# Output projection of a fused two-block kernel: two tiles move ahead of the last transposes of attention, and the sums of squares follow two tiles behind instead of one

## The chip, the cores and the metric

The kernel runs on one core of one Trainium2 chip. The metric is the time of one execution on the device, in microseconds (us). Three executions were timed before the change: 3608.86, 3610.43 and 3611.48 us, median 3610.43 us. One more execution was recorded by the profiler; its own time was 3605.72 us and the span from its first to its last instruction 3604.4 us.

## What is computed

Two transformer blocks, each on 1024 tokens of width 1024, all in fp32. The first mixes tokens with grouped attention, a Hyena convolution and differential attention, projects the result with `w_out`, adds it (scaled by a gate) to the residual and goes into a gated MLP. The second is a three-part attention mixer and a mixture of experts. The change lies in the step of the first block between attention and MLP:

```python
def merge_groups(ya, yh, yd, g_out, w_out, lam_init):
    ya = rms_norm(ya, g_out[:A_WIDTH])
    yh = rms_norm(yh, g_out[A_WIDTH:A_WIDTH + HY_WIDTH])
    yd = rms_norm(yd, g_out[A_WIDTH + HY_WIDTH:].reshape(D_HEADS, D_VALUE_DIM)) * (1.0 - lam_init)
    return jnp.concatenate([ya, yh, yd.reshape(b, n, D_WIDTH)], axis=-1) @ w_out
...
# then, in the block: x = x + gate * y; h = rms_norm(x, norm2_g), modulated; the MLP reads h
```

## The kernel before, in words

Every engine has its own generator of instructions (`pe_...`, `act_...`, `dve_...`, `sp_...`). A generator yields the name of an event that it needs, such as `("yt", 7, 1)`, and gets the semaphore and the count to wait for; so the order on each engine is the order of its own code, and only semaphores tie the engines together. Two of the tools matter here: `claim(b)` makes TensorE wait until PSUM bank `b` has been read by its last user (`held[b]`), and `ring` hands out banks in turn.

**Attention** works through 48 units: for each of 8 query tiles of 128 tokens two units of grouped attention and four of differential attention. When a query tile `qt` is complete, it is normalised in small steps between the units: VectorE copies the Hyena part in (L1148), ScalarE squares and sums six groups (L1086), takes a reciprocal square root (L302, L304, each with a table load), VectorE refines it (L308 to L312) and scales the six groups (L1161, event `("yn", qt)`). Then TensorE turns the eight 128x128 blocks of the tile to feature-major layout (`pe_features`, L1032, in two PSUM banks), and ScalarE copies them to `YT` with the output gain (`act_norm`, L1098, event `("yt", qt, h2)`). For the last query tile, 7, there are no more units between which these steps could go. A query tile of the Hyena part lands on every second token, tiles 0 to 3 and 4 to 7 in the first and in the second 512 tokens.

**Output projection** (`pe_wout`). There are 16 tiles of 128 features x 512 tokens, in the order of `halves`: the first 512 tokens (tc = 0) for features 0 to 7, then the second 512. They are called T0 to T15 here. A tile is 8 matmuls in the code, each of which the profile shows as two rows (fp32), so 16 rows on L1237; it goes to the next of banks 0 to 5. T0 to T7 read only the first 512 columns of `YT`. VectorE then adds the tile, times the gate, to the residual (`dve_wout`, L1253, event `xadd`), which SyncE loads from DRAM in eight transfers of 512 KB (L1197, `xres`) into memory that held the attention's operands. ScalarE squares the sum (`act_wout`, L1272, event `rsq`) into one of two buffers that it uses in turn; TensorE adds the squares over the features with a matmul by a constant (`pe_wout_sum` by way of `pe_column_sum`, L1221, two rows, event `rss`), into bank 6 for the first token half and bank 7 for the second. These are called S0 to S15. In the order before, S(i-1) stands behind Ti. When S7 is there, VectorE and ScalarE make the factors of the first half (L1256, L302, L304, L308 to L312) and the normalised input of the MLP (L1261, L1278), and only then go on with T8; likewise after S15, on which the MLP (`pe_glu`, L1298) waits.

**Weights** come in chunks of 1 MB through four slots (L197); a chunk of `w_out` serves two tiles. The first two chunks are loaded during attention, the third and fourth when the last attention unit no longer reads their slots. SyncE then waits for `("yt", 7, 1)`, issues the eight residual loads, and goes on with the chunks for T8 to T15.

The lines of the order before: TensorE waits for `("yt", 7, 1)` ahead of all tiles (L1230), `pe_features(7, ttb)` ends `pe_attention` (L1055).

Of the kernel before, what the change touches and what calls it, by code (L numbers as in the profile page):

```python
# [85 lines left out]
class Turns:  # L86
# [9 lines left out]
    def turn(self, *events):  # L96
        i = self.i
        self.i = (i + 1) % len(self.sems)
        self.counts[i] += 16
        for event in events:  # L100
            self.engine.at[event] = (self.sems[i], self.counts[i])
        return self.sems[i], 16
# [21 lines left out]
def build(nc, X, out):  # L124
# [4 lines left out]
    V, A, G, P, S = (Engine(nc, e, n, at) for e, n in ((vt, "dve"), (st, "act"), (gt, "pool"), (nc.tensor, "pe"), (dma, "sp")))  # L129
# [3 lines left out]
    def sb(off, n, p0=0, p1=128):  # L133
        assert off + n <= TOTAL
        return arena[p0:p1, off:off + n]
# [13 lines left out]
    def bk(b, n=512, p0=0, p1=128, off=0):  # L149
        return psum[p0:p1, b, off:off + n]  # L150
# [14 lines left out]
    def claim(*banks):  # L165

        for b in banks:
            for event in held[b]:
                P.wait_ge(*(yield event))
            held[b] = []  # L170

    def ring(ids):
        i = 0
        while True:
            yield ids[i % len(ids)]
            i += 1
# [8 lines left out]
    def wat(n):  # L185
        return M_WR + (n % NWR) * WSZ

    def wready(n):
        return wsem[n % NWR], 16 * (n // NWR + 1)
# [770 lines left out]
    def grouped(i):  # L960
        return i is not None and 0 <= i < NU and units[i][0] == "a"
# [13 lines left out]
    def norm_step(i):  # L975
        return divmod(i - 8, 6) if i > 7 else (0, -1)

    def pe_scores(i):
        kind, qt, h = units[i]
        q, key = (QA, KA) if kind == "a" else (QD, KD + h * 1280)  # L980
        yield from claim(*range(6))
        for c, n in ((0, 512), (512, 512), (1024, 256)):
            for j in range(2):
                ins = mm(bk(3 * j + c // 512, n), sb(q + h * 1024 + qt * 128, 128, 64 * j, 64 * j + 64), sb(key + c, n, 64 * j, 64 * j + 64), True, True)  # L984
                if c == 1024:
                    ins.then_inc(*P.step(("score", i, j)))
        for b in range(6):
            held[b] = [("cmax", i, b // 3)]

    def pe_turn(i, j, ttb):  # L990
        P.wait_ge(*(yield ("exp", i, 1) if units[i][0] == "a" else ("comb", i)))
        for g in range(3):
            b = next(ttb)
            yield from claim(b)
            for k in range(4 * g, min(10, 4 * g + 4)):
                ins = turn(bk(b, 128, off=k % 4 * 128), prob(i, j)[:, k * 128:k * 128 + 128], ident)  # L996
            bank[("turn", i, j, g)] = b
            ins.then_inc(*P.step(("turn", i, j, g)))
            held[b] = [("pt", i, j, g)]

    def pe_values(i, ttb):
        kind, qt, h = units[i]
        b = next(ttb)
        yield from claim(b)
        for j in range(2 if kind == "a" else 1):
            P.wait_ge(*(yield ("pt", i, j, 2)))
        for k in range(10):
            if kind == "a":
                for j in range(2):
                    ins = mm(bk(b, 128, 64 * j, 64 * j + 64), sb(VA + k * 128 + 64 * j, 64), probt(i, j, k * 128, 128), k == 0, k == 9)  # L1010
            else:
                ins = mm(bk(b, 128), probt(i, 0, k * 128, 128), sb(VD + k * 512 + h * 128, 128), k == 0, k == 9)  # L1012
        bank[("val", i)] = b
        ins.then_inc(*P.step(("val", i)))
        held[b] = [("yt4", i) if kind == "a" else ("y", i)]

    def pe_back(i, ttb):
        b = next(ttb)
        yield from claim(b)
        P.wait_ge(*(yield ("yt4", i)))  # L1020
        bank[("back", i)] = b
        turn(bk(b, 128), sb(YA, 128), ident).then_inc(*P.step(("back", i)))
        held[b] = [("y", i)]

    def pe_features(qt, ttb):
        y = YTK + qt % 2 * 1024
        P.wait_ge(*(yield ("yn", qt)))
        for h2 in range(2):
            b = next(ttb)
            yield from claim(b)  # L1030
            for k in range(4):
                ins = turn(bk(b, 128, off=k * 128), sb(y + (4 * h2 + k) * 128, 128), ident)  # L1032
            bank[("feat", qt, h2)] = b
            ins.then_inc(*P.step(("feat", qt, h2)))
            held[b] = [("yt", qt, h2)]

    def pe_attention():
        ttb = ring([6, 7])
        P.wait_ge(*(yield ("lam",)))
        P.wait_ge(*(yield ("qv", NJ - 1)))  # L1040
        P.wait_ge(*(yield ("qk", roped[-1])))
        for i in range(NU + 3):
            if i < NU:
                yield from pe_scores(i)
            if 2 <= i < NU + 2:
                yield from pe_turn(i - 2, 0, ttb)
            if i > 2:
                yield from pe_values(i - 3, ttb)
            if grouped(i - 4):
                yield from pe_back(i - 4, ttb)  # L1050
            if grouped(i - 2):
                yield from pe_turn(i - 2, 1, ttb)
            if norm_step(i)[1] == 5:
                yield from pe_features(norm_step(i)[0], ttb)
        yield from pe_features(7, ttb)  # L1055

    def act_turn(i, j):
        x = side_of[i, j]
# [130 lines left out]
    halves = [(tc, f) for tc in range(2) for f in range(8)]  # L1189
# [27 lines left out]
    def pe_column_sum(tile, ready, done, tc, f):  # L1217
        if f == 0:
            yield from claim(6 + tc)
        P.wait_ge(*(yield ready))  # L1220
        mm(bk(6 + tc), con("o1024"), tile, f == 0, f == 7).then_inc(*P.step(done))  # L1221

    def pe_wout_sum(tc, f):
        yield from pe_column_sum(sb(SQ + f % 2 * 512, 512), ("rsq", tc, f), ("rss", tc, f), tc, f)
        if f == 7:
            held[6 + tc] = [("rx", tc)]

    def pe_wout():
        banks = ring(range(6))
        P.wait_ge(*(yield ("yt", 7, 1)))  # L1230
        for tc, f in halves:
            n = nth["wout"][4 * tc + f // 2]
            b = next(banks)
            yield from claim(b)
            P.wait_ge(*wready(n))
            for k in range(8):
                ins = mm(bk(b), sb(wat(n) + k * 256 + f % 2 * 128, 128), sb(YT + k * 1024 + tc * 512, 512), k == 0, k == 7)  # L1237
            bank[("wout", tc, f)] = b
            ins.then_inc(*P.step(("wout", tc, f), *([("w", n)] if f % 2 else [])))
            held[b] = [("xadd", tc, f)]  # L1240
            if f:
                yield from pe_wout_sum(tc, f - 1)
            elif tc:
                yield from pe_wout_sum(0, 7)
        yield from pe_wout_sum(1, 7)

    def dve_wout():
# [1503 lines left out]
    def pe_program():  # L2751
        P.stage("front")
        yield from pe_front()
        P.stage("hyena")
        yield from pe_hyena()
        P.stage("qkv")
        yield from pe_qkv()
        P.stage("attention")
        yield from pe_attention()
        P.stage("ffn")  # L2760
        yield from pe_wout()
        yield from pe_glu()
        yield from pe_down()
        P.stage("band")
        yield from pe_band()
        P.stage("mla")
        yield from pe_mla()
        P.stage("wout2")
        yield from pe_wout2()
        yield from pe_route()  # L2770
        P.stage("experts")
        yield from pe_experts()
        yield from pe_final()
# [247 lines left out]
```

## Time and profile before

| what | value |
|---|---|
| three executions, median (lowest to highest) | 3610.43 us (3608.86 to 3611.48) |
| profiled execution, its own time | 3605.72 us |
| its span | 3604.4 us |
| TensorE busy with matmuls | 3410.5 us, 95% of the span |
| VectorE, ScalarE, GpSimd busy | 1569.7, 901.0, 261.8 us |
| mean granted TensorE clock | 0.98 of full speed |
| output projection, first row of L1237 to last of L1221 | 1058.4 to 1193.4 us |

The profile gives each instruction's start and duration, what the engine waited for ahead of it, and the granted TensorE clock; a matmul of one row is about 0.43 us from the last at 512 columns and full clock. The ends of matmuls are modelled and overlap the next start a little, so pitches are read from starts.

### The profile page before, as it was taken

The page shows a single profiled execution, that of the slowest core. Times are in us where ns is not written, and L with a number is a line of the kernel's source. Part 1 is how long each engine was busy: PE and PEld are TensorE (multiplying, and loading weights), DVE is VectorE, ACT ScalarE, POOL GpSimd, SP SyncE. Part 2 cuts the span into 40 slices and gives each one's busy share as a digit, 9 for nine tenths or more (in the row PEclk, how much of TensorE's full clock was granted, in tenths as well). Part 3 has the DMA queues.
Part 4 walks back from the last instruction along what each step waited for, and adds up shares of the span by engine and source line. Part 5 has one row for each costly group of instructions (what it writes and reads, how often), then busy time and mean ns, then how long its engine had stood idle before and what let it go on. Part 6 is the DMA issues. An engine that isn't in the chain of part 4 may idle for free.

```text
span 3604.4 us, 30844 instructions
## 1 busy us (share of the span) xinstructions
PE 3410.5 (95%) x12338; PEld 1861.5 (52%) x12338; DVE 1569.7 (44%) x2766; ACT 901.0 (25%) x1750; POOL 261.8 (7%) x251
## 2 busy tenths in 40 slices
PE   8999998899989899999999999999999987999997
PEld 3458545666654344444444555765457434444443
DVE  6355476466631555554543213314666133211114
ACT  4110363377751100000000112213334121111112
POOL 0012232000000000000000000000000002222221
PEclk9999999999999999999999999999999998999999
DMA  6124212000022211110210200002000108999994
GB/s 231 35 70 160 98 47 105 24 1 1 1 82 82 70 38 45 47 47 29 87 47 24 85 24 30 31 7 91 12 24 1 49 24 353 370 370 366 370 369 168
DMA packets 63242, 370.56 MB, mean 103 GB/s; under 512 B 6826, under 2 KB 13242, under 8 KB 37500
## 3 DMA queue, kind: packets, MB, share of 16 engines
q1 hardware_dynamic: 40492, 187.71, 14.3%
q0 software_dynamic: 22608, 180.89, 13.3%
q8 instruction: 97, 1.59, 0.2%
q14 instruction: 45, 0.37, 0.0%
HBM read 329.16 MB, written 39.41 MB: 102 GB/s over the span
## 4 chain that ended last, share of the span: by engine, by line
PE 83%; DVE 7%; ACT 7%; DMA 1%; issue 1%; SPq 0%; POOL 0%; DVEq 0%; ACTq 0%; POOLq 0%
PE ps L1298 15%; PE ps L2568 9%; PE ps L1421 7%; PE ps L1596 6%; PE ps L2587 4%; PE ps L837 3%; PE ps L2225 3%; PE ps L1237 3%; PE ps L1598 3%; PE ps L984 2%; PE ps L703 2%; PE ps L840 2%; PE ps L1012 2%; PE ps L646 2%; ACT arena L1064 2%; PE ps L2065 2%
## 5 line engine op out<-in xcount | busy, mean ns | idle before, releaser
L1298 PE MATMUL ps<-arena 128*128 128x512 f32 x1232 | 532.1, 594 | 9.4 <-DVE arena L1324 9.4
L1298 PEld LDWEIGHTS ps<-arena 128*128 128x128 f32 x1232 | 234.3, 190 | 307.0 <-issue 287.1
L2568 PE MATMUL ps<-arena 128*128 128x512 f32 x752 | 331.1, 593 | 0.0
L1421 PE MATMUL ps<-arena 128*128 128x512 f32 x616 | 264.6, 592 | 0.0
L2526 POOL DMA_INDIRECT arena<-in_wgu_dram,arena x47 | 44.2, 940 | 2639.7 <-DVE arena L2485 2387.5
L2568 PEld LDWEIGHTS ps<-arena 128*128 128x128 f32 x752 | 139.6, 191 | 157.7 <-issue 157.7
L1596 PE MATMUL ps<-arena 128*128 128x512 f32 x480 | 209.1, 596 | 0.0
L1421 PEld LDWEIGHTS ps<-arena 128*128 128x128 f32 x616 | 116.6, 189 | 147.9 <-issue 143.8
L1119 DVE TENSOR_SCALAR_CACHE_REDUCE arena<-ps 128x1280 f32<-128x1280 f32 x96 | 139.3, 1488 | 110.1 <-PE ps L984 110.1
L837 PE MATMUL ps<-arena 128*128 128x512 f32 (+1 forms) x432 | 174.7, 558 | 0.0
L2587 PE MATMUL ps<-arena 128*128 128x512 f32 x376 | 169.1, 592 | 0.5 <-DVE arena L2638 0.5
L2642 DVE TENSOR_TENSOR arena<-arena,ps 128x256 f32<-128x256 f32 x47 | 19.8, 421 | 323.6 <-ACT arena L2613 323.6
L1596 PEld LDWEIGHTS ps<-arena 128*128 128x128 f32 x480 | 90.8, 190 | 113.8 <-issue 113.8
L1077 ACT ACTIVATE arena<-arena 128x1280 f32<-128x1280 f32 x96 | 129.5, 1353 | 7.0 <-DVE arena L1119 7.0
L984 PE MATMUL ps<-arena 64*128 64x512 f32 (+1 forms) x576 | 119.7, 547 | 6.8 <-DVE arena L1119 3.1
L837 PEld LDWEIGHTS ps<-arena 128*128 128x128 f32 x432 | 82.1, 191 | 84.7 <-issue 82.5
L1613 DVE COPY arena<-ps 128x512 f32<-128x512 f32 (+2 forms) x31 | 16.6, 536 | 247.5 <-PE ps L1596 157.7
L996 PE MATMUL ps<-arena 128*128 128x128 f32 x640 | 100.0, 285 | 24.3 <-ACT arena L1064 21.0
L2587 PEld LDWEIGHTS ps<-arena 128*128 128x128 f32 x376 | 71.4, 190 | 90.2 <-issue 89.4
L1237 PE MATMUL ps<-arena 128*128 128x512 f32 x256 | 115.9, 607 | 1.4 <-ACT arena L1098 1.4
L1064 ACT ACTIVATE arena<-ps 128x512 f32<-128x512 f32 (+1 forms) x192 | 93.8, 523 | 85.9 <-PE ps L996 83.5
L2225 PE MATMUL ps<-arena 128*128 128x512 f32 x256 | 112.5, 592 | 0.7 <-DVE arena L2195 0.7
(375 smaller groups left out, 4940.9 us busy)
## 6 DMA issues: line engine op xcount, KB each, us to landing
arena<-in_wmod_dram SPq DMA_DIRECT2D x24, 1024.0 KB, 5.5
yslot<-arena SPq DMA_DIRECT2D x47, 512.0 KB, 9.1
arena<-in_wup_dram SPq DMA_DIRECT2D x22, 1024.0 KB, 4.8
arena<-in_wout_dram SPq DMA_DIRECT2D x16, 1024.0 KB, 4.8
arena<-in_cf_dram SPq DMA_DIRECT2D x12, 1024.0 KB, 4.8
arena<-in_wdn_dram SPq DMA_DIRECT2D x16, 704.0 KB, 4.0
arena<-in_w2b_dram SPq DMA_DIRECT2D x9, 1024.0 KB, 4.8
arena<-in_ci_dram SPq DMA_DIRECT2D x16, 512.0 KB, 3.5
```

What stands on the lines that cost most here:

```text
L837: ins = mm(bk(b, size), sb(wat(n) + k * 256 + col, 128), x, k == 0, k == 7)
L984: ins = mm(bk(3 * j + c // 512, n), sb(q + h * 1024 + qt * 128, 128, 64 * j, 64 * j + 64), sb(key + c, n, 64 * j, 64 * j + 64), True, True)
L1064: st.activation(probt(i, j, g * 512, n), bk(bank[("turn", i, j, g)], n), ACT.Copy).then_inc(*A.step(("pt", i, j, g)))
L1077: st.activation(prob(i, j), prob(i, j), ACT.Exp, bias=stat(i, f"bias{j}"), scale=-1.0, accum_out=stat(i, f"sum{j}")).then_inc(*A.step(("ex ...
L1119: vt.tensor_scalar(prob(i, j), scores(j), -SCALE, None, MUL, ALU.min, accum_out=stat(i, f"bias{j}")).then_inc(*V.step(("cmax", i, j)))
L1237: ins = mm(bk(b), sb(wat(n) + k * 256 + f % 2 * 128, 128), sb(YT + k * 1024 + tc * 512, 512), k == 0, k == 7)
L1298: ins = mm(bk(b), left[:, k], right[:, k], k == 0, k == 3)
L1421: ins = mm(bk(b), sb(left + k * 128, 128), right(k), k == 0, k == 10)
L1596: ins = mm(bk(b), sb(w, 128), sb(x + tile * 512, 512), k == 0, k == 7)
L2225: ins = mm(bk(b), sb(wat(n) + k * 256 + f % 2 * 128, 128), sb(OF + k * 1024 + tc * 512, 512), k == 0, k == 7)
L2568: ins = mm(bk(b), sb(XB + i % 2 * 1024 + k * 128, 128), sb(WGU[i % 3] + k * 512, 512), k == 0, k == 7)
L2587: ins = mm(bk(6 + h2), sb(HB + 512 + i % 2 * 256 + k * 128, 128), sb(WDN[i % 4] + k * 1024 + h2 * 512, 512), k == 0, k == 1)
```

## The change

TensorE's order alone changes. The transposes of query tile 7 leave the end of `pe_attention` and stand behind T1; T0 to T7 wait for query tile 6 (`("yt", 6, 1)`) instead of 7, T8 to T15 still for tile 7; the transposes take a new ring of banks 6 and 7. S(i-2) instead of S(i-1) stands behind Ti, from T2 on, and S14 and S15 close the projection. The code of the other engines is the same.

```diff
                 yield from pe_turn(i - 2, 1, ttb)
             if norm_step(i)[1] == 5:
                 yield from pe_features(norm_step(i)[0], ttb)
-        yield from pe_features(7, ttb)
...
     def pe_wout():
         banks = ring(range(6))
-        P.wait_ge(*(yield ("yt", 7, 1)))
-        for tc, f in halves:
+        for i, (tc, f) in enumerate(halves):
+            P.wait_ge(*(yield ("yt", 7 if tc else 6, 1)))
             n = nth["wout"][4 * tc + f // 2]
             b = next(banks)
             yield from claim(b)
...
             held[b] = [("xadd", tc, f)]
-            if f:
-                yield from pe_wout_sum(tc, f - 1)
-            elif tc:
-                yield from pe_wout_sum(0, 7)
+            if i == 1:
+                yield from pe_features(7, ring([6, 7]))
+            if i > 1:
+                yield from pe_wout_sum(*halves[i - 2])
+        yield from pe_wout_sum(1, 6)
         yield from pe_wout_sum(1, 7)
```

One line falls away above `pe_wout`, so the line numbers behind it are lower by one after the change.

TensorE, from the values of the last attention unit (L1012) on, before. L1032 are the transposes, L1237 the projection, L1221 the sums; `attention_act` and `ffn_act` are ScalarE's semaphores, `attention_dve` and `ffn_dve` VectorE's, `weights0` to `weights3` the four slots:

```order
L1012 MATMUL ps<-arena 128x128 [waits attention_act]
L1012 MATMUL ps<-arena 128x128 x9
L1032 MATMUL ps<-arena 128x128 [waits attention_act,attention_dve]
L1032 MATMUL ps<-arena 128x128 x7
L1237 MATMUL ps<-arena 128x512 [waits weights0,attention_act]
L1237 MATMUL ps<-arena 128x512 x15
L1221 MATMUL ps<-arena 128x512 [waits ffn_act]
L1237 MATMUL ps<-arena 128x512 [waits weights1]
L1237 MATMUL ps<-arena 128x512 x7
L1221 MATMUL ps<-arena 128x512 [waits ffn_act]
```

And the same place after:

```order
L1012 MATMUL ps<-arena 128x128 [waits attention_act]
L1012 MATMUL ps<-arena 128x128 x9
L1236 MATMUL ps<-arena 128x512 [waits weights0,attention_act]
L1236 MATMUL ps<-arena 128x512 x15
L1031 MATMUL ps<-arena 128x128 [waits attention_dve]
L1031 MATMUL ps<-arena 128x128 x7
L1236 MATMUL ps<-arena 128x512 [waits weights1]
L1236 MATMUL ps<-arena 128x512 x7
L1220 MATMUL ps<-arena 128x512 [waits ffn_act,attention_act]
L1236 MATMUL ps<-arena 128x512 x8
```

T0 and T1 (x16 matmuls) went ahead of the eight transposes, and S0 went from behind T1 to behind T2, where it also waits for ScalarE's reading of the bank that the transposes used.

TensorE at the end of the projection, where L1298 (L1297 after) is the first product of the MLP, before:

```order
L1221 MATMUL ps<-arena 128x512 [waits ffn_act]
L1237 MATMUL ps<-arena 128x512 [waits ffn_dve]
L1237 MATMUL ps<-arena 128x512 x7
L1221 MATMUL ps<-arena 128x512 [waits ffn_act] x2
L1298 MATMUL ps<-arena 128x512 [waits weights0,ffn_dve]
```

And after:

```order
L1220 MATMUL ps<-arena 128x512 [waits ffn_act]
L1236 MATMUL ps<-arena 128x512 [waits ffn_dve]
L1236 MATMUL ps<-arena 128x512 x7
L1220 MATMUL ps<-arena 128x512 [waits ffn_act] x3
L1297 MATMUL ps<-arena 128x512 [waits weights0,ffn_dve]
```

Three sums instead of two stand behind T15.

## Rows read from the trace of the kernel before

**Rows 1.** The page: busy time of the engines, and the chain that ended last.
```profile
PE 3410.5 (95%) x12338; PEld 1861.5 (52%) x12338; DVE 1569.7 (44%) x2766; ACT 901.0 (25%) x1750; POOL 261.8 (7%) x251
...
PE 83%; DVE 7%; ACT 7%; DMA 1%; issue 1%; SPq 0%; POOL 0%; DVEq 0%; ACTq 0%; POOLq 0%
```

**Rows 2.** Waits of TensorE, 1040 to 1200 us: us in total, times, longest.
```profile
PE ps L1032 <- DVE arena L1161: 8.9, 1, 8.9
PE ps L1221 <- ACT arena L1272: 6.1, 2, 5.5
PE ps L1237 <- ACT arena L1098: 1.4, 1, 1.4
```

**Rows 3.** Timeline of TensorE: start, us, instructions [idle before <- releaser].
```profile
1041.83 1.27 PE L1032 MATMUL ps<-arena 128*128 128x128 f32 x8
1043.67 2.50 PE L1012 MATMUL ps<-arena 128*128 128x128 f32 x20 [0.57 <-ACT arena L1098]
1055.04 1.97 PE L1032 MATMUL ps<-arena 128*128 128x128 f32 x8 [8.88 <-DVE arena L1161]
1058.42 16.73 PE L1237 MATMUL ps<-arena 128*128 128x512 f32 x32 [1.41 <-ACT arena L1098]
1074.99 1.02 PE L1221 MATMUL ps<-arena 128*128 128x512 f32 x2
1075.85 7.03 PE L1237 MATMUL ps<-arena 128*128 128x512 f32 x16
1082.71 1.02 PE L1221 MATMUL ps<-arena 128*128 128x512 f32 x2
```

**Rows 4.** Stretches: us, busy us (x) by engine, then PEclk, DMA share, GB/s.
```profile
1046.20:1055.00 8.80, 0.00 (x0) 0.00 (x0) 3.06 (x14) 5.61 (x16) 0.00 (x0) 0.73 0.64 238
1058.40:1062.00 3.60, 3.58 (x5) 1.51 (x6) 0.00 (x0) 0.00 (x0) 0.00 (x0) 0.50 0.73 229
1062.00:1064.00 2.00, 2.00 (x4) 0.97 (x3) 0.00 (x0) 0.00 (x0) 0.00 (x0) 0.51 1.01 399
```

**Rows 5.** Timeline of ScalarE, VectorE and SyncE's queue around the first tiles.
```profile
1042.47 2.18 ACT L1098 ACTIVATE arena<-ps,arena 128x128 f32<-128x128 f32 x8 [2.75 <-PE ps L1032]
1056.19 2.18 ACT L1098 ACTIVATE arena<-ps,arena 128x128 f32<-128x128 f32 x8 [3.45 <-PE ps L1032]
...
1068.40 0.75 DVE L1253 SCALAR_TENSOR_TENSOR arena<-ps,arena 128x512 f32<-128x512 f32 x1 [13.41 <-PE ps L1237]
...
1069.19 0.63 ACT L1272 ACTIVATE arena<-arena 128x512 f32<-128x512 f32 x1 [10.82 <-DVE arena L1253]
...
1058.40 3.76 SPq L1197 DMA_DIRECT2D arena<-in_xT_dram  x8
```

**Rows 6.** TensorE at S8, between the halves, and at the end of the projection.
```profile
1142.41 2.08 PE L1221 MATMUL ps<-arena 128*128 128x512 f32 x2 [5.45 <-ACT arena L1272]
1144.28 7.83 PE L1237 MATMUL ps<-arena 128*128 128x512 f32 x16
...
1190.58 1.02 PE L1221 MATMUL ps<-arena 128*128 128x512 f32 x2
1192.24 1.13 PE L1221 MATMUL ps<-arena 128*128 128x512 f32 x2 [0.65 <-ACT arena L1272]
```

**Rows 7.** Residual loads: the issues at 1058.8 and 1059.2; then landing of all.
```profile
L1197 SPq DMA_DIRECT2D arena<-in_xT_dram x2: 431/432/432, 1058.8 to 1059.2; - x2
...
DMA to landing us min/median/max: 5.5/5.5/5.5
...
DMA to landing us min/median/max: 5.5/7.5/9.4
```

**Rows 8.** The page: issues of `w_out` chunks, KB each, median us to landing.
```profile
arena<-in_wout_dram SPq DMA_DIRECT2D x16, 1024.0 KB, 4.8
```

**Rows 9.** TensorE after a short wait late in attention, 1033 to 1038 us.
```profile
1033.44 0.69 PE L996 MATMUL ps<-arena 128*128 128x128 f32 x2 [2.06 <-ACT arena L1064]
1033.93 3.78 PE L1012 MATMUL ps<-arena 128*128 128x128 f32 x20
```

## The prediction

> **What bounds the kernel.** First the page: TensorE is busy 95% of the span, and the chain that ended last runs through it for 83% [rows 1]. VectorE and ScalarE are busy 44% and 25%, so they matter only where TensorE waits for them. Hence the second view, TensorE's waits in the stretch of the change. There are four in 160 us that cost a microsecond or so: 8.9 us ahead of the last transposes, for VectorE's scaling of query tile 7; 1.4 us ahead of T0, for ScalarE's copies of those transposes; and 5.5 us and 0.65 us ahead of S8 and S15, for squares [rows 2, 6]. Third, the timeline gives their places [rows 3]: the last values of attention end at 1043.67 + 2.50 = 1046.17 us, the transposes begin at 1055.04, T0 at 1058.42, T2 at 1075.85. Fourth, the granted clock [rows 4]: over the wait it falls from full to half (mean 0.73 over 1046.2 to 1055.0), and is still at 0.50 in T0's first 3.6 us and 0.51 in the 2 us behind. These are the levels of 1.2 and 2.4 GHz.
>
> Everything behind the projection (MLP, band attention, routing, experts) is released by its result, in the same order on all engines. So what TensorE gains up to S15 should reach the end, unless a transfer or the clock takes it back.
>
> **The wait ahead of the transposes.** T0 and T1 need the first 512 tokens of `YT` (query tile 6 and those before it), their first weights, and banks 0 and 1. Tile 6's copies end at 1042.47 + 2.18 = 1044.65 us [rows 5]; the weights were loaded during attention; the banks were last read by the maxima of the last scores, long before the values. So T0 can start when the values end, at 1046.1. The idle 8.88 us are filled.
>
> T0 and T1 take two tiles at full clock. A warm tile is 1082.71 - 1075.85 = 6.86 us, two are 13.72 [rows 3]. They end at about 1059.9, later than 1055.0, when tile 7 is ready, so the transposes wait for nothing. The clock was full ahead of 1046 (20 rows in 2.50 us, which took 3.78 us at the low clock [rows 3, 9]) and finds no idle stretch now. Before, the pair took 1074.99 - 1058.42 = 16.57. Gain 2.85 us. The transposes took 1.97 us slow and 1.27 us for tile 6 at full clock [rows 3]: gain 0.70 us.
>
> **The wait ahead of T0.** The 1.41 us for ScalarE's copies are gone: what follows the transposes now is T2, which needs only tile 6 and its weights. Gain 1.41 us.
>
> **What becomes later.** The transposes run at 1059.9 instead of 1055.0. The copies start when the first four are done, at about 1060.5 (0.64 us behind, as 1042.47 - 1041.83 shows), and end 2.18 us later at 1062.7; before, at 1058.4. SyncE's queue waits for just this with the eight residual loads, and behind them the weights of T8 to T15. These move by 4.3 us against the clock on the wall, and by some 19 us against T2, which starts at 1061.2 instead of 1075.85. For the weights that is covered: T8 begins some 46 us after T2, and such a chunk lands in 4.8 us [rows 8]. For the residual it has to be worked out, because S0 stands behind T2 and needs load, addition and square of T0. T2 ends at 1061.2 + 6.86 = 1068.0. The third load, issued at 1059.24, landed 5.5 us later at 1064.7 [rows 7]; loads follow each other at 512 KB / 399 GB/s = 1.3 us [rows 4], so the first landed about 2.6 us before it, at 1062.1, or 3.7 us after the first issue. Now that is 1062.7 + 3.7 = 1066.4; addition 0.75 and square 0.63 us, with 0.04 us between each [rows 5], give 1067.9. The stall at S0 is about nothing; I take 0.1 us. The bounds are 0 and what it would be if the first load took as long as the last, 9.4 us [rows 7]: 5.6 us. From S1 on there is a whole tile more.
>
> **Sums two behind.** No sum is added or removed; each is 0.86 us (1075.85 - 1074.99). Ahead of T15's end there is one fewer (S0 to S12 instead of S0 to S13), behind it one more. Before, S15 began 1192.24 - 1190.58 = 1.66 us after T15's end, 0.65 us of it idle while T15's addition and square ran [rows 6]. Now S13 and S14, 1.72 us, stand there and fill the idle time; the square also waits for S13, since there are two buffers, but that ends 0.86 us in, about when the addition ends. Gain 0.86 - 0.06 = 0.80 us.
>
> The wait at S8 I leave as it is. It comes from VectorE, which makes the first half's norm between S7 and T8's addition. Before, the order is S7, T9, S8; now S7, T10, S8. One tile lies between in both, so 5.45 us stay, with the slow clock behind it: S8 takes 2.08 and the next tile 7.83 us [rows 6]. Banks don't change that: T14, the first tile to reuse T8's, comes four tiles after T10.
>
> ScalarE's squares get a later release: the square of Ti needs S(i-2), now issued behind Ti instead of T(i-1). That is ready 0.86 us after Ti, the addition 0.8 to 0.95 us after it, so nothing moves, and the result is needed a tile later than before.
>
> **Sum.** 8.88 + 1.41 + 2.85 + 0.70 + 0.80 - 0.1 = 14.5 us. Against the profiled execution: 3605.72 - 14.5 = 3591.2 us. That execution was 4.7 us faster than the median of the three timed ones (3610.43) and below the fastest, so for a timed median I take 3610.4 - 14.5 = **3595.9 us**.
>
> **The clock, weighed.** After a wait of 2.06 us, 20 rows took 3.78 instead of 2.50 us [rows 3, 9]; after the 0.57 us ahead of the values nothing slowed; after the 5.45 us at S8 the loss was 1.22 + 0.80 = 2.0 us; after 8.88 and 1.41 us, 3.55 us. So the loss isn't in proportion to the wait. The Trainium skill, "TensorE: Matmul & The Clock Gate", section "What's actually happening", says that the window in which activity is judged runs freely and doesn't restart with the kernel's work, so where a stretch lies in it decides how much runs slow. By that rule the waits behind the projection, all moved by 14.5 us, may each cost a little more or less than in this trace, and the sum would be 14.5 give or take a few us rather than 14.5. No row here shows the same wait at two phases, only unequal losses.
>
> **Rivals.**
> 1. *The residual comes late.* S0 waits for the first load as if it took the last's 9.4 us: 5.6 us, and such a wait brings 2 us of slow clock, as at S8. Gain 14.5 - 5.5 - 2.0 = 7.0, time 3603.4; halfway it is 3599.6. For it: the third load took 5.5 us, and this is the one place where slack falls from a tile and more to about zero. Against it: loads land at an even spacing, which puts the first at 3.7 us. Chance 0.10.
> 2. *The clock takes or gives.* The later waits meet the clock otherwise. By the losses above each moves by up to 2 us; three in one direction make 6 us: 3602 or 3590. For it: the unequal losses. Against: signs should differ. Chance 0.06.
> 3. *It does nothing:* T0 does not start early, because a count it waits for is reached only with tile 7. Then T0 would wait as before; 3610. Against it: the wait is for tile 6's copies, and ScalarE ran them before the values ended [rows 5]. Chance 0.03.
> 4. *Slower.* The two square buffers tie TensorE and ScalarE together: a sum finds its square not made and waits for the chain addition, square, that behind T15 is 1.66 us from the tile's end [rows 6]. At 15 sums that is 24.9 us; less 14.5 it is 10.4 slower, 3620.8. It decides against the change if more than 8 to 9 of the sums wait so. Against it: the chain is 1.7 us long and S(i-2) comes more than 14 us after its tile's end (two tiles). Chance 0.01.
>
> **How the numbers follow.** A measurement of this kernel can tell about 0.2%, or 7.2 us, from no change; faster means below 3603.2. The forecast has 0.80; its own range, with 2 us on each side for the clock and 1.5 us for executions (they spread by 2.6 us), is 3592.5 to 3599.5. The rivals 1 and 2 reach to 3603.4 and 3590. For 8 in 10 with some doubt about my own terms I give 3591.5 to 3602.0. Faster 0.80 + 0.09 + 0.05 = 0.94; same 0.01 + 0.01 + 0.03 = 0.05; slower 0.01.
>
> **What the profile after would show.** T0 starting within 0.3 us of the values' end, at clock 1.00; transposes with no wait of VectorE, taking about 1.3 us; no wait ahead of T2; S0 waiting under 0.5 us; S8 waiting about 5.5 us still, some 14 us earlier; three sums in a row at the end with no idle time; S15 at about 1177.7 instead of 1192.2. Wrong would be: a wait of microseconds at S0, T0 at a low clock, or a projection that ends 14 us sooner while the whole is not 14 us shorter.

## The result, and the profile after

The changed kernel's five timed executions have a median of 3590.9 us (3589.77 to 3594.19), five of before in the same job 3610.43 us (3608.37 to 3611.48). The ratio is 0.9944, with a 95% interval of 0.9934 to 0.9955. The profiled execution took 3590.90 us, its span 3589.6 us. That is 14.8 us less than the profiled execution of before, but 19.5 us less between the medians. The forecast was 3595.9 us. It was right in direction and, as the rows below show, in what happens in the projection; the result lies 5.0 us under it and 0.6 us under the lower end of its range, 3591.5. What is to be explained is therefore not the projection but these 5 us.

The page of the changed kernel, to be read against [rows 1]:

```profile
PE 3406.6 (95%) x12338; PEld 1858.3 (52%) x12338; DVE 1569.4 (44%) x2766; ACT 900.4 (25%) x1750; POOL 261.8 (7%) x251
```

The same instructions; TensorE is busy 3.9 us less, since fewer of them run at the low clock. The other 10.9 us of the span were idle time.

TensorE's timeline of the changed kernel, in the columns of [rows 3, 6]. L1236 is the projection, L1220 the sums, and the row of x8 at 128x128 the transposes. These are on L1032 and the MLP's first product is on L1298, as before; the lists of the order ahead of the prediction, which give L1031 and L1297 for them, are one line off:

```profile
1042.61 2.50 PE L1012 MATMUL ps<-arena 128*128 128x128 f32 x20 [0.57 <-ACT arena L1097]
1044.94 13.90 PE L1236 MATMUL ps<-arena 128*128 128x512 f32 x32
1058.68 1.04 PE L1032 MATMUL ps<-arena 128*128 128x128 f32 x8
1059.55 7.03 PE L1236 MATMUL ps<-arena 128*128 128x512 f32 x16
1066.74 1.10 PE L1220 MATMUL ps<-arena 128*128 128x512 f32 x2 [0.15 <-ACT arena L1272]
...
1121.76 7.03 PE L1236 MATMUL ps<-arena 128*128 128x512 f32 x16
1134.24 2.08 PE L1220 MATMUL ps<-arena 128*128 128x512 f32 x2 [5.45 <-ACT arena L1272]
1136.11 7.96 PE L1236 MATMUL ps<-arena 128*128 128x512 f32 x16
...
1174.81 2.93 PE L1220 MATMUL ps<-arena 128*128 128x512 f32 x6
1177.58 7.03 PE L1298 MATMUL ps<-arena 128*128 128x512 f32 x16
```

T0 follows the values without a wait and at full clock (32 rows from 1044.94 to 1058.68, 13.74 us); the transposes wait for nobody; S0 waits 0.15 us; S8 waits the same 5.45 us; S13, S14 and S15 (x6) stand in a row with no idle time, and the MLP begins at 1177.58 instead of 1193.21. The start of the last values and the start of the MLP's first product bound the stage that the change touches. I use that stage from here on: 1193.21 - 1043.67 = 149.5 us before, 1177.58 - 1042.61 = 135.0 us after, **14.6 us less**; the sum had said 14.5.

The residual loads and the first additions of the changed kernel, SyncE's queue and VectorE's timeline:

```profile
1061.51 3.84 SPq L1196 DMA_DIRECT2D arena<-in_xT_dram  x8
...
1065.18 0.75 DVE L1253 SCALAR_TENSOR_TENSOR arena<-ps,arena 128x512 f32<-128x512 f32 x1 [11.26 <-DMA arena<-in_xT_dram]
1066.46 0.75 DVE L1253 SCALAR_TENSOR_TENSOR arena<-ps,arena 128x512 f32<-128x512 f32 x1 [0.52 <-DMA arena<-in_xT_dram]
```

The first two additions now wait for the loads; before, the first one waited for T0 [rows 5]. The first can start 1065.18 - 1061.51 = 3.67 us after the first issue, the second 1.28 us later: the worked-out 3.7 and 1.3.

### The profile page after: what moved, and what is told of

It reads as the page before. It is cut to its first block, busy times and chain, and to the rows that moved or that the text cites. A ratio compares the mean times of both kernels' runs of the same rounds, so it can differ in the third digit from the quotient of the medians.

```text
span 3589.6 us, 30844 instructions
## 1 busy us (share of the span) xinstructions
PE 3406.6 (95%) x12338; PEld 1858.3 (52%) x12338; DVE 1569.4 (44%) x2766; ACT 900.4 (25%) x1750; POOL 261.8 (7%) x251
## 4 chain that ended last, share of the span: by engine, by line
PE 83%; DVE 8%; ACT 7%; issue 1%; DMA 1%; SPq 0%; another core or an unknown queue 0%; POOL 0%; DVEq 0%; ACTq 0%
PE ps L1298 15%; PE ps L2568 9%; PE ps L1421 7%; PE ps L1596 6%; PE ps L2587 5%; PE ps L837 3%; PE ps L2225 3%; PE ps L1598 3%; PE ps L1236 3%; PE ps L984 2%; PE ps L703 2%; PE ps L840 2%; PE ps L1012 2%; PE ps L646 2%; ACT arena L1063 2%; PE ps L2065 2%
## 5 line engine op out<-in xcount | busy, mean ns | idle before, releaser
L1298 PE MATMUL ps<-arena 128*128 128x512 f32 x1232 | 532.5, 594 | 9.4 <-DVE arena L1324 9.4
L1298 PEld LDWEIGHTS ps<-arena 128*128 128x128 f32 x1232 | 234.5, 190 | 307.3 <-issue 287.4
L1421 PE MATMUL ps<-arena 128*128 128x512 f32 x616 | 264.7, 592 | 0.0
L1596 PE MATMUL ps<-arena 128*128 128x512 f32 x480 | 209.1, 596 | 0.0
L1421 PEld LDWEIGHTS ps<-arena 128*128 128x128 f32 x616 | 116.6, 189 | 147.8 <-issue 143.8
L1596 PEld LDWEIGHTS ps<-arena 128*128 128x128 f32 x480 | 90.7, 190 | 113.9 <-issue 113.9
L1236 PE MATMUL ps<-arena 128*128 128x512 f32 x256 | 113.2, 596 | 0.0
L2225 PE MATMUL ps<-arena 128*128 128x512 f32 x256 | 112.5, 592 | 0.7 <-DVE arena L2195 0.7
```

The costliest lines, as they stand in the source:

```text
L1298: ins = mm(bk(b), left[:, k], right[:, k], k == 0, k == 3)
L1421: ins = mm(bk(b), sb(left + k * 128, 128), right(k), k == 0, k == 10)
L1596: ins = mm(bk(b), sb(w, 128), sb(x + tile * 512, 512), k == 0, k == 7)
```

## Experiments

**Theories.** The gain of a kernel is told in two ways below: by its stage in one profile, and by whole executions against those of before in the same job, a set of executions on one chip. A: the change is worth its stage, 14.5 us, and the rest of the difference between medians is the draw of executions. B: the wait ahead of the transposes costs the clock more in most executions than in the profiled one. C: the sums' delay brings only its 0.8 us. D, formed after the first two jobs: the change gains another 2 us or more outside its stage in every execution.

**Copies of both kernels, first job.** No edit.

> The kernel of before, word for word. Theory A (the change is worth 14.5 us in every execution, and the timed medians of 3610.4 and 3590.9 us, 19.5 us apart, differ further because executions draw their slow-clock stretches at random): ratio 1.000, executions spread over 3605 to 3612 us, and their granted clock falls as their time rises. Theory B (the 8.9 us wait ahead of the last transposes costs the clock more in most executions than the 3.5 us of the profiled one): median again near 3610, and the profile of this run shows a longer stretch at the low clock around T0 than 13.65 us.

> The changed kernel, word for word. Theory A: the median gain over before in this job falls anywhere from 14 to 19 us, since it is 14.5 plus the luck of both sides. Theory B: it is again 18 to 21 us.

Measured: the copy of before 3607.70 us median of 11 against 3607.65 of 21 for before, ratio 1.0003 (0.9994 to 1.0012); stage 1195.04 - 1045.47 = 149.6 us, with a slow stretch as long as in the first profile (T0 and T1 took 16.74 us), which gives nothing to B. The copy of the changed kernel: 3592.05 us, ratio 0.9958 (0.9945 to 0.9972), 15.6 us; stage 135.0 us. This spoke for A.

**The clock's share alone.** The kernel of before, with 10 matmuls (20 rows) put into the long wait; nobody reads their result.

```diff
+        yield from claim(5)
+        P.wait_ge(*(yield ("yt", 6, 1)))
+        for k in range(10):
+            mm(bk(5), con("o1024"), sb(YT + k % 8 * 1024, 512), True, True)
         yield from pe_features(7, ttb)
```

> The order of before, with 10 matmuls of 128x512 into a free bank (8.6 us, their result is not read) between the last values of attention and the transposes of query tile 7, so that TensorE is busy in the wait but nothing moves. It measures the clock's share alone. Theory A: transposes and T0, T1 run at full clock, gain 3.5 us, 3607. Theory B: gain 7 to 9 us, 3602.

Measured: 3605.87 us, ratio 0.9996 (0.9987 to 1.0005), so for the whole kernel no gain is shown. TensorE's timeline of this kernel (L1058 is the filler):

```profile
1042.94 2.50 PE L1012 MATMUL ps<-arena 128*128 128x128 f32 x20 [0.57 <-ACT arena L1102]
1045.27 8.75 PE L1058 MATMUL ps<-arena 128*128 128x512 f32 x20
1054.31 1.10 PE L1032 MATMUL ps<-arena 128*128 128x128 f32 x8 [0.29 <-DVE arena L1165]
1057.24 14.00 PE L1241 MATMUL ps<-arena 128*128 128x512 f32 x32 [1.83 <-ACT arena L1102]
...
1189.17 7.03 PE L1302 MATMUL ps<-arena 128*128 128x512 f32 x16
```

Kept busy, TensorE stays at full clock: T0 and T1 take 14.00 instead of 16.73 us, the transposes 1.10 instead of 1.97, the stage 1189.17 - 1042.94 = 146.2 us, 3.3 us less than before, where 3.5 were expected; T0 waits 1.83 instead of 1.41 us, since the transposes end sooner and ScalarE's copies do not. So of the stage's 14.6 us, about 3.3 are the clock's. B's 7 to 9 us are out.

**Only T0 and T1 ahead, sums one behind.** Against the changed kernel:

```diff
-            if i > 1:
-                yield from pe_wout_sum(*halves[i - 2])
-        yield from pe_wout_sum(1, 6)
+            if i > 0:
+                yield from pe_wout_sum(*halves[i - 1])
         yield from pe_wout_sum(1, 7)
```

> Of the change only the first part: T0 and T1 ahead of the transposes, but S(i-1) behind Ti as before, so S0 stands right behind the transposes. Theory A (the stage from the start of the last values to the MLP's first product, 149.5 us before and 135.0 after, holds the whole effect; the rest of the difference between medians is the draw of executions): S0 waits about 7 us for the first residual load, addition and square, with 2 us of slow clock, stage 144 us, so 5.3 us less than before. Rival C (the sums' delay brings only its 0.8 us at the end): stage near 136.

Measured: 3603.51 us, ratio 0.9981 (0.9972 to 0.9990). TensorE's timeline:

```profile
1043.89 2.50 PE L1012 MATMUL ps<-arena 128*128 128x128 f32 x20 [0.57 <-ACT arena L1097]
1046.23 13.90 PE L1236 MATMUL ps<-arena 128*128 128x512 f32 x32
1059.96 1.04 PE L1032 MATMUL ps<-arena 128*128 128x128 f32 x8
1068.11 2.04 PE L1220 MATMUL ps<-arena 128*128 128x512 f32 x2 [7.11 <-ACT arena L1271]
1069.95 7.58 PE L1236 MATMUL ps<-arena 128*128 128x512 f32 x16
...
1188.95 7.03 PE L1297 MATMUL ps<-arena 128*128 128x512 f32 x16
```

S0 waits 7.11 us for the square, since the residual loads now start only behind the transposes, and the clock falls again. The stage is 145.1 us, 4.5 us less than before and 10.1 more than with both parts. It was expected at 144. C is out: the second part of the change is what lets the first part's gain through.

**Only the sums two behind.** The kernel of before, with the loop counted by `i` as in the change, and nothing moved but the sums.

```diff
-            if f:
-                yield from pe_wout_sum(tc, f - 1)
-            elif tc:
-                yield from pe_wout_sum(0, 7)
+            if i > 1:
+                yield from pe_wout_sum(*halves[i - 2])
+        yield from pe_wout_sum(1, 6)
         yield from pe_wout_sum(1, 7)
```

> Of the change only the second part: transposes where they were, the wait for query tile 7 ahead of T0, S(i-2) behind Ti. Both theories: the waits of 8.88 and 1.41 us and the slow clock stay, 0.8 us are won at the end: stage 148.7 us, ratio 0.9998, no difference that can be measured.

Measured: 3605.96 us, ratio 0.9989 (0.9980 to 0.9998). The stage, from TensorE's rows below, is 1191.32 - 1042.55 = 148.8 us, 0.8 us less as expected. But the ratio was expected at 0.9998, and the whole gained about 4 us; that is outside the stage.

```profile
1042.55 2.50 PE L1012 MATMUL ps<-arena 128*128 128x128 f32 x20 [0.57 <-ACT arena L1098]
1053.93 1.97 PE L1032 MATMUL ps<-arena 128*128 128x128 f32 x8 [8.88 <-DVE arena L1161]
...
1188.55 2.93 PE L1221 MATMUL ps<-arena 128*128 128x512 f32 x6
1191.32 7.03 PE L1297 MATMUL ps<-arena 128*128 128x512 f32 x16
```

**One tile ahead instead of two.** Against the changed kernel:

```diff
-            if i == 1:
+            if i == 0:
                 yield from pe_features(7, ring([6, 7]))
```

> The changed kernel with only T0 ahead of the transposes, T1 behind them. T0 ends 2.0 us before VectorE has scaled query tile 7, so TensorE waits 2 us there; the residual loads start 4 us earlier and S0 doesn't wait. Theory A: stage 135.0 + 2.0 - 0.2 = 136.8 us at full clock, up to 138.3 if a wait of 2 us brings the slow clock as it did at 1033 us in the kernel before (1.3 us lost).

Measured: 3595.67 us, ratio 0.9962 (0.9948 to 0.9975). TensorE's timeline:

```profile
1043.03 2.50 PE L1012 MATMUL ps<-arena 128*128 128x128 f32 x20 [0.57 <-ACT arena L1097]
1045.36 7.03 PE L1236 MATMUL ps<-arena 128*128 128x512 f32 x16
1054.40 1.09 PE L1032 MATMUL ps<-arena 128*128 128x128 f32 x8 [2.01 <-DVE arena L1160]
1055.33 13.90 PE L1236 MATMUL ps<-arena 128*128 128x512 f32 x32
...
1136.50 2.08 PE L1220 MATMUL ps<-arena 128*128 128x512 f32 x2 [5.46 <-ACT arena L1272]
1138.37 9.01 PE L1236 MATMUL ps<-arena 128*128 128x512 f32 x16
...
1180.89 7.03 PE L1298 MATMUL ps<-arena 128*128 128x512 f32 x16
```

The 2.01 us wait is there and S0 has none. The clock did not fall behind it (x32 in 13.90 us), while a wait of 2.06 us in [rows 9] brought it down. Instead the tile behind S8 took 9.01 us, against 7.83 and 7.96 us in the kernels before and after, behind the same 5.45 us wait. The stage is 137.9 us, between the 136.8 and 138.3 us that were expected, but the time beyond 136.8 was lost at S8 and not behind the new wait.

**The wait at S8 taken out.** On top of the change, VectorE adds T8 and T9, and ScalarE squares them, before the first half's norm is refined.

```diff
             vt.tensor_scalar(sb(r + 512, 512), bk(6 + tc), 1.0, EPS, MUL, ADD).then_inc(*V.step(("rx", tc)))
+            if tc == 0:
+                yield from dve_xadd(1, 0)
+                yield from dve_xadd(1, 1)
...
             yield from act_rsqrt(sb(r, 512), sb(r + 512, 512), ("rx", tc), ("re", tc))
+            if tc == 0:
+                yield from act_square(1, 0)
+                yield from act_square(1, 1)
```

(`dve_xadd` and `act_square` are the loop bodies of before, which now leave out those two tiles.)

> The changed kernel, and besides VectorE adds T8 and T9 and ScalarE squares them before the first half's norm is refined (in the 2.64 us in which VectorE waits for the reciprocal root), so that S8 finds its square made. Both theories: the 5.45 us wait at S8 and 2.0 us of slow clock behind it go, 7.5 us less than the changed kernel. If VectorE's norm then comes too late for a later tile's bank or square, a wait shows up at S10 or T14 instead and less than 4 us are won.

Measured: 3585.52 us, ratio 0.9943 (0.9930 to 0.9957), where the copy of the changed kernel in the same job had 0.9958 (0.9945 to 0.9972). TensorE's timeline:

```profile
1044.77 2.50 PE L1012 MATMUL ps<-arena 128*128 128x128 f32 x20 [0.57 <-ACT arena L1097]
...
1123.98 7.03 PE L1236 MATMUL ps<-arena 128*128 128x512 f32 x16
1130.85 1.02 PE L1220 MATMUL ps<-arena 128*128 128x512 f32 x2
1131.71 7.03 PE L1236 MATMUL ps<-arena 128*128 128x512 f32 x16
...
1169.48 2.93 PE L1220 MATMUL ps<-arena 128*128 128x512 f32 x6
1172.25 7.03 PE L1312 MATMUL ps<-arena 128*128 128x512 f32 x16
```

No wait is left at S8 (1130.85) and none shows up later; the stage is 127.5 us, 7.5 less than the changed kernel's, as worked out.

**And the MLP's first wait shortened.** On top of the last edit, VectorE makes the MLP's first weight sums while it waits for the reciprocal root of the second half.

```diff
                 yield from dve_xadd(1, 1)
+            else:
+                yield from dve_weight_sums(0)
...
-        yield from dve_weight_sums(0)
         yield from dve_token_sums()
```

> The changed kernel with T8 and T9 added and squared ahead of the first half's norm (as in the run before, stage 127.5 us), and besides the MLP's first weight sums made by VectorE while it waits for the second half's reciprocal root. The stage up to the MLP's first product stays at 127.5 us; the wait of 9.45 us in the MLP's first block shrinks to about 7.2 us, bound then by ScalarE's last shift of the normalised input. Whole kernel 9 to 10 us less than the changed kernel, near 3583.

Measured: 3585.43 us, ratio 0.9931 (0.9917 to 0.9944), the best of all ratios. The wait in the MLP's first block is 7.36 us; it is 9.45 us in the kernel of the last edit, whose row stands first:

```profile
1188.73 26.44 PE L1312 MATMUL ps<-arena 128*128 128x512 f32 x54 [9.45 <-DVE arena L1338]
...
1172.22 7.03 PE L1314 MATMUL ps<-arena 128*128 128x512 f32 x16
1186.60 28.73 PE L1314 MATMUL ps<-arena 128*128 128x512 f32 x61 [7.36 <-DVE arena L1340]
```

The median was expected at 3583; the 2.4 us that are missing lie where the next section finds those that the changed kernel has too many.

**Copies of both, second job,** to decide between A and D. No edit.

> The changed kernel again, one of three copies in a job with a copy of before, to tell a gain of 14.5 us that is the stage's alone (theory A) from one of about 17 to 19 us to which the change adds 2 us or more elsewhere in every execution (theory D, as the medians so far hint: 19.5, 15.6). Theory A: median gain against before 12 to 17 us, the mean of the three copies 13.5 to 16; stage 135.0 us in the profile.

> As the run before: theory A 12 to 17 us, theory D 17 to 19 us; stage 135.0 us, and what lies outside the stage between 3452 and 3460 us as in all profiles so far.

> The kernel of before again. Both theories: ratio within 0.0008 of 1, which shows how far two sets of executions of the same kernel lie apart; stage 149.5 us.

> As the first and second of this job: theory A 12 to 17 us, theory D 17 to 19 us; stage 135.0 us.

Measured: the three copies of the changed kernel 3591.27, 3592.85 and 3594.46 us, ratios 0.9940, 0.9942 and 0.9943 (together from 0.9926 to 0.9956); before 3612.5 us (15 executions), its copy 3610.85 us, ratio 0.9993 (0.9984 to 1.0002). The gains against before are 18 to 21 us, against its copy 16 to 20; A had said 12 to 17 and D 17 to 19. The stages are 149.9 us for the copy of before and 135.3, 135.0 and 135.4 us for the others: 14.7 us between their means. Outside the stage the changed kernel's profiles have 3454.3, 3455.1 and 3460.3 us, the last a little more than the 3460 that were expected at most. Of all executions in all jobs, copies and profiled ones among them, 85 of before have a mean of 3609.9 us and 25 of the changed kernel 3592.7 us: **17.2 us**. The jobs differ: before has means of 3608.5, 3610.2 and 3611.6 us in the three later ones, copies included. Against before in its own job the changed kernel gained 18.3, 16.5 and 18.4 us between means. Each is more than A's 14.5, so A is out. D's direction holds: some 2 to 4 us come from outside the stage, and the profiles say where 2.6 of them are.

## Why the prediction was wrong by a little

**Where the 2.6 us are.** I cut each profile at the first starts of lines behind the stage, and compared these pieces.

| piece behind the stage (first start to first start) | before, 3 profiles | changed, 5 profiles |
|---|---|---|
| band attention and its projections (L1596 to L1904) | 509.7, 509.7, 509.6 | 508.1, 508.0, 508.0, 508.1, 508.2 |
| MLA attention (L2065 to L2225) | 225.9, 225.8, 225.8 | 224.5, 224.6, 224.7, 224.5, 224.6 |
| MLP (L1298 to L1421) | 541.4, 541.4, 541.4 | 541.8, 541.7, 541.9, 541.8, 542.0 |

All engines execute the same instructions there. In no piece do the two kernels overlap, and together they make 1.6 + 1.3 - 0.4 = 2.5 us. Inside the first piece TensorE's timeline of the kernel before has this:

```profile
2440.74 0.66 PE L1654 MATMUL ps<-arena 128*128 128x128 f32 x4 [1.19 <-ACT arena L1713]
2441.33 1.32 PE L1641 MATMUL ps<-arena 64*128 64x128 f32 x8
2442.59 3.49 PE L1667 MATMUL ps<-arena 128*128 128x128 f32 x16
2445.87 0.84 PE L1654 MATMUL ps<-arena 128*128 128x128 f32 x4
```

and of the changed kernel, at the same place of the program:

```profile
2425.56 0.66 PE L1654 MATMUL ps<-arena 128*128 128x128 f32 x4 [1.19 <-ACT arena L1713]
2426.15 1.32 PE L1641 MATMUL ps<-arena 64*128 64x128 f32 x8
2427.40 2.05 PE L1667 MATMUL ps<-arena 128*128 128x128 f32 x16
2429.29 0.60 PE L1654 MATMUL ps<-arena 128*128 128x128 f32 x4
```

The same wait of 1.19 us stands ahead of both. Behind it 16 rows take 3.49 us in one and 2.05 us in the other. The stretches of 10 us around them, before and then after, have the granted clock in the third column from the right:

```profile
2440.00:2450.00 10.00, 9.26 (x56) 8.31 (x58) 5.16 (x12) 4.65 (x21) 0.00 (x0) 0.83 0.26 82
```

```profile
2425.00:2435.00 10.00, 9.41 (x69) 8.21 (x70) 6.33 (x14) 5.32 (x23) 0.00 (x0) 1.00 0.40 140
```

So the clock falls to 1.2 GHz for a few microseconds at this wait in all three profiles of before, and in none of the five of the changed kernel; row by row, all of the band piece's 1.6 us arise here.

In the MLA piece, 0.7 of the 1.3 us arise in the same way behind another wait. Before, and then the changed kernel:

```profile
2700.98 0.48 PE L2077 MATMUL ps<-arena 128*128 128x128 f32 x1 [1.71 <-ACT arena L2112]
2701.25 1.92 PE L2053 MATMUL ps<-arena 96*128 96x512 f32 x2
```

```profile
2683.51 0.33 PE L2077 MATMUL ps<-arena 128*128 128x128 f32 x1 [1.81 <-ACT arena L2112]
2683.68 1.39 PE L2053 MATMUL ps<-arena 96*128 96x512 f32 x2
```

Another 0.5 us come from a slow stretch at the start of the piece, which reaches less far into it in the changed kernel. The MLP's 0.4 us the other way arise behind its 9.45 us wait, where the changed kernel is slow for a row more.

The prediction had cited the Trainium skill, "TensorE: Matmul & The Clock Gate", section "What's actually happening", that activity is judged in a window that runs freely. If so, whether a short wait is caught depends on when it comes. The trace agrees in so far as the same 1.19 us wait had two outcomes; that its place in such a window decided, no run here shows. The outcome was not drawn anew in each execution either: in these pieces the same kernel met the same slow stretches in every profile. Nor does the size of the shift foretell it. With only the sums moved, 0.8 us in the stage, the band and MLA pieces take 508.1 and 224.5 us as after the change; with one tile ahead, 11.7 us, they take 509.4 and 225.5 us and with both waits out, 21.9 us, 509.7 and 225.9 us, nearly or just as before.

**It fits the other kernels too.** The gain of the stage plus that of the pieces from the MLP to the step ahead of the experts (L1298 to L2557), against how far the mean of each kernel's executions lies below 3609.9 us. The gains in the first row are between the means of the profiles, in the others between the kernel's one profile and the first of before:

| kernel | stage | behind it | sum | executions |
|---|---|---|---|---|
| changed | 14.6 | 2.6 | 17.2 | 17.2 |
| only the sums two behind | 0.8 | 2.9 | 3.7 | 4.1 |
| only T0 and T1 ahead | 4.5 | 2.4 | 6.9 | 6.3 |
| one tile ahead | 11.7 | 1.8 | 13.5 | 13.6 |
| filler in the wait | 3.3 | 0.4 | 3.7 | 3.5 |
| S8's wait out | 22.1 | 2.0 | 24.1 | 23.6 |
| both waits out | 21.9 | 2.2 | 24.1 | 24.4 |

In the last line 2.1 of the 2.2 us are the edit's own, in the MLP; its band piece takes 509.7 us as before. That is why it stayed 2.4 us above what was expected. Every sum is within 0.6 us of the last column. That column takes all jobs together for before; against before in its own job the filler kernel gained 2.0 us and the one with S8's wait out 22.1 us, 1.7 and 2.0 us less than their sums, and the other four edited kernels 4.4, 6.6, 13.9 and 24.7 us. So the sums hold to about 2 us, not to 0.6. The parts ahead of the stage and from the experts on are left out, as if they were alike in the mean.

**Point by point.**

- *The wait ahead of the transposes, 8.88, 0.70 and 2.85 us:* right. T0 starts at the values' end at full clock, the pair takes 13.74 us (13.72 forecast). The transposes take 0.87 us from start to start where 1.27 were counted, so 0.4 us more came from them, and 0.16 us more from the wait, since the modelled end of the values lies behind the point at which T0 starts.
- *The wait ahead of T0, 1.41 us:* right; T2 waits for nothing.
- *S0's stall, 0.1 us between 0 and 5.6:* 0.15 us in the first profile, 0.17 to 0.35 in the copies; from start to start T2 and S0 together took 8.13 us instead of 7.72. The first load's 3.7 us held at 3.67. Rival 1 was wrong.
- *Sums two behind, 0.80 us:* right, 0.8 us alone (148.8 against 149.5). What the prediction did not say is what they are worth together with the rest: without them S0 waits 7.11 us and the stage is 10.1 us longer.
- *S8's wait stays:* right, 5.45 us in all. The next tile took 7.96 instead of 7.83 us. The prediction's loss of 1.22 us for S8 sets its length, 2.08 us, against a pitch of 0.86; like with like (1.02) it is 1.06 us, and with the tile's 0.80 the loss is 1.9 us and not 2.0. With S8's wait taken out the stage still fell by the 7.5 us that were worked out.
- *The sum of 14.5 us for the stage:* measured 14.6 us in the first profile and between the means. That it agrees to 0.1 us is partly luck: 0.4 and 0.2 us too little were counted at the front, and 0.3 at S0, 0.1 at the tile behind S8 and 0.1 at the end too much.
- *3591.2 us for the profiled execution:* it took 3590.9, and that is luck. Beside the stage's 14.6 us it gained 1.1 us ahead of it and 2.8 us between the MLP and the experts, and lost 3.6 us from the experts on.
- *From what base:* "for a timed median I take 3610.4 - 14.5". The base was fair: 85 executions have a mean of 3609.9 us.
- *The clock behind the projection:* this is **the step that failed**. The prediction said that the waits behind the projection, all moved by 14.5 us, may each cost a little more or less, "14.5 give or take a few us"; but it put 0 for them in the sum, and allowed 2 us to each side in its own range. This term measured 2.6 us in the changed kernel's favour, between the means of three and five profiles. With it the sum is 3609.9 - 14.6 - 2.6 = 3592.7 us, the mean of 25 executions. The rest is the draw of the first five executions: their median, 3590.9, lies 1.8 us below that mean, within the spread of executions (3589.0 to 3597.0). So of the 5.0 us between forecast and result 2.6 are this term, 1.8 the draw, 0.5 the base and 0.1 the stage. The lower end, 3591.5, had room for one of the first two, but both in one direction reach it, and the small ones go past it; rival 2, "the clock takes or gives", covered it down to 3590 but with a chance of only 0.06.
- *Rivals 3 and 4:* out by the first rows of the profile after.

What stays open: why the slow stretches of these pieces fall alike in executions of one kernel, and how one could foretell them. They don't fall alike everywhere: what lies ahead of the stage varies by up to 5 us between profiles of one kernel (the last values start between 1042.6 and 1048.2 us), and what follows from the experts on (L2557) by up to 4 us (599.9 to 603.6 us before, 601.5 to 603.8 us after the change). Neither was followed up. In the means of the profiles the changed kernel has 1.8 us less ahead of the stage and 1.5 us more from the experts on; that these cancel is a reason to trust the table's sums no further than a microsecond or two.

## What to carry to other kernels

Where an in-order engine waits at a seam between two stages, look for pieces of the next stage that depend only on the last but one step, put them ahead of the late work, and then ask what their consumers wait for: here the residual load starts behind the late work, so the fill paid 4.5 us with the sums close behind and 14.6 us with the sums one tile further back. Price such a seam as the idle time plus the slow clock behind it (3.3 us of 14.6 here), and check it on the stage, start to start, which varied by at most 0.4 us between profiles of one kernel, while whole executions of before spread over nearly 14 us (3604.3 to 3618.0). For the whole kernel give the range a few microseconds more in both directions, because moving everything behind the seam can add or remove slow stretches at short waits far away.

## What the hardware showed that I had not expected

- The same wait can cost nothing or 1.4 us: behind 1.19 us in band attention, 16 rows took 3.49 us before and 2.05 us after the change. A wait of 2.06 us in [rows 9] was followed by the slow clock and one of 2.01 us in the kernel with one tile ahead was not; other work stands around these two.
- In the pieces between the MLP and the experts this is not noise from execution to execution. It came out alike in three of three profiles of one kernel and five of five of the other, so some 2.6 us of a measured gain can belong to a change without coming from any instruction that it touched.
- With 20 rows of filler in the 8.88 us wait the clock stays up, and the stage is 3.3 us shorter without moving any work. In the whole kernel this did not show: the ratio was 0.9996 (0.9987 to 1.0005), and its band piece took 511.3 us, 1.6 us more than before.
